# Attention values of two heads side by side in TensorE's column halves

## The reference

```
h  = rms_norm(x) * (1 + scale) + shift            # also for the context tokens
p  = h @ w_in                                     # 1024 x 2336, split among groups A, B, C, D
oA = softmax(qA kA^T / 8) vA                      # grouped keys: 4 query heads, 2 key/value heads
oB = softmax(qB kB^T / sqrt(96)) vB               # latent attention, 4 heads
oC = softmax over a window of +-128 tokens, the context keys and a sink logit, grouped keys
oD = softmax(qD kD^T / 8 + bias of a neighbourhood) vD
x  = x + gate * rms_norm(concat(oA, oB, oC, oD) @ w_out)
```

## Time and profile before

| | |
|---|---|
| median of 3 runs | 3002.4 us |
| profiled execution, its own time | 2995.0 us |
| its span | 2993.2 us |
| TensorE busy | 2667.0 us (89%), 13395 instructions |
| weight loads busy | 1353.2 us (45%) |
| VectorE busy | 1127.2 us (38%) |
| ScalarE busy | 576.0 us (19%) |
| GpSimd busy | 389.7 us (13%) |
| mean granted TensorE clock | 0.951 |
| from HBM and to it | 219 GB/s over the span |

### The profile page before, as it was taken

One profiled execution on the slowest core, in us unless ns is written; L12 is line 12 of the kernel. 1 busy time (PEld: TensorE's weight loads), 2 busy tenths in 40 slices (PEclk: granted clock), 3 DMA queues, 4 the chain that ended last, 5 costly groups with the idle time before them and its releaser, 6 DMA issues. The chain is left out here.

```text
span 2993.2 us, 44262 instructions
## 1 busy us (share of the span) xinstructions
PE 2667.0 (89%) x13395; PEld 1353.2 (45%) x13396; DVE 1127.2 (38%) x3287; ACT 576.0 (19%) x1309; POOL 389.7 (13%) x312
## 2 busy tenths in 40 slices
PE   7999989896899999999997598999978999899994
PEld 3576665653433333333332266666633333333331
DVE  3443361523433333333332653451524232333323
ACT  2222231311011111111111331331311111111111
POOL 1000001001012222222221200001010112122121
PEclk9999999997999999999998799999989999999997
DMA  7120203014577998999993502102137799998983
GB/s 273 43 88 29 100 28 127 13 43 162 217 242 254 357 332 287 325 321 333 328 362 88 194 1 88 70 30 111 36 137 282 293 395 393 384 402 288 384 329 105
DMA packets 104978, 619.26 MB, mean 207 GB/s; under 512 B 22832, under 2 KB 23088, under 8 KB 64688
## 3 DMA queue, kind: packets, MB, share of 16 engines
q1 hardware_dynamic: 71184, 530.30, 44.9%
q0 software_dynamic: 33696, 87.63, 12.0%
HBM read 578.84 MB, written 77.99 MB: 219 GB/s over the span
## 5 line engine op out<-in xcount | busy, mean ns | idle before, releaser
L1518 PE MATMUL ps<-wgu,xT 128*64 128x512 f32 x3584 | 810.9, 606 | 49.8 <-DMA wgu<-in_exp_gu 33.0
L1518 PEld LDWEIGHTS ps<-wgu,xT 128*64 128x64 f32 x3584 | 255.5, 139 | 510.1 <-issue 498.4
L1527 PE MATMUL ps<-wd,hiddenT 128*64 128x512 f32 x1824 | 418.3, 600 | 11.3 <-issue 10.3
L624 PE MATMUL ps<-w_in,hT 128*128 128x512 f32 (+5 forms) x1152 | 371.4, 482 | 14.8 <-PEq L381 4.0
L1447 POOL DMA_INDIRECT ffn_rows<-Y,six x114 | 182.5, 1601 | 1119.2 <-issue 649.7
L1700 DVE TENSOR_TENSOR hidden<-silu,ps 128x256 f32<-128x256 f32 x112 | 47.2, 421 | 713.3 <-ACT silu L1636 713.3
L624 PEld LDWEIGHTS ps<-w_in,hT 128*128 128x128 f32 x1152 | 218.2, 197 | 157.2 <-issue 137.8
L1527 PEld LDWEIGHTS ps<-wd,hiddenT 128*64 128x64 f32 x1824 | 123.8, 137 | 225.3 <-issue 224.3
L1636 ACT ACTIVATE silu<-ps 128x256 f32<-128x256 f32 x112 | 43.1, 384 | 807.1 <-PE ps L1518 807.1
L1694 DVE TENSOR_SCALAR Y<-ps,wc 128x512 f32<-128x512 f32 x114 | 85.6, 751 | 198.0 <-PE ps L1527 198.0
L1631 ACT ACTIVATE Y<-ps,wc 128x512 f32<-128x512 f32 x114 | 78.4, 688 | 415.7 <-PE ps L1527 415.7
(11 more groups left out here) (470 smaller groups left out, 2915.6 us busy)
## 6 DMA issues: line engine op xcount, KB each, us to landing
wgu<-in_exp_gu SPq DMA_DIRECT2D x128, 2048.0 KB, 13.5
wd<-in_exp_d SPq DMA_DIRECT2D x128, 1024.0 KB, 12.8
ada_start<-in_ada_w SPq DMA_DIRECT2D x8, 1024.0 KB, 7.9
w_in<-in_w_in SPq DMA_DIRECT2D x4, 2048.0 KB, 10.1
w_in<-in_w_out SPq DMA_DIRECT2D x4, 2048.0 KB, 12.6
aw_0A<-in_ada_w SPq DMA_DIRECT2D x6, 1024.0 KB, 5.4
aw_0B<-in_ada_w SPq DMA_DIRECT2D x6, 1024.0 KB, 4.8
aw_0C<-in_ada_w SPq DMA_DIRECT2D x6, 1024.0 KB, 4.9
```

The source lines that it names most:

```text
L624: last = pe.matmul(pp[i % 2][:, at:at + c1 - c0], hT[:, k, i * P:(i + 1) * P], wg[g % 2][:, k, c0:c1], start=(k == 0), stop=(k == KD - 1))
L1518: last = pe.matmul(ps[h * HB:(h + 1) * HB, 0, :], xT[:, k, h * HB:(h + 1) * HB], wgu[w[h]][:, k, :], start=(k == 0), stop=(k == KD - 1))
L1527: last = pe.matmul(ps[h * HB:(h + 1) * HB, 1 + c, :], G[:, f, h * HB:(h + 1) * HB], wd[w[h]][:, f, c * 512:(c + 1) * 512], start=(f == 0), ...
```

## The change

Units are reordered so that two heads of the same query tile follow each other, and each two make a pair `w`. `values(w)` treats both: V is stationary (64 columns), the turned probabilities move (128 columns), and the two heads go to the two column halves, that is to partitions 0 to 63 and 64 to 127 of one bank. The output so has head columns on partitions and query tokens along the row, which is the form that the output projection reads. The inverse sums lie one per partition (query token); they are spread by two more products (a broadcast column stationary, the identity moving), copied by ScalarE to RB, and VectorE multiplies and writes to `oT`, which is held for all tiles. PT has four buffers in place of two; PR takes the storage of R. In `project_out` the turns and their copies go. The host reorders rows of `w_out` to fit the order of heads in A and C.

```diff
+    units = [(2 * p + side, q) for p in range(2) for q in range(nt) for side in range(2)]
+    pairs = [(units[2 * w][0] // 2, units[2 * w][1]) for w in range(NU // 2)]
...
+        PR, PT = R, sb("PT", [P, 4, 768])
+        RB = sb("RB", [P, P])
...   in turn_probs(u):
-                    s_o.wait(pe, u - 1)
+                    if u % 2:
+                        s_o.wait(pe, u // 2)
...
-                def values(u):
-                    s_pa.wait(pe, local[u])
-                    s_pd.wait(pe, u + 1)
-                    c0 = kv_of(units[u][0]) * HD
-                    for c in range(lo(u) // P, 6):
-                        last = pe.matmul(ps[:, 5 + 2 * (u % 2), 256:256 + HD], PT[:, u % 2, c * P:(c + 1) * P],
-                                         V[:, key_tile(u, c), c0:c0 + HD], start=(c == lo(u) // P), stop=(c == 5))
+                def values(w):
+                    q = pairs[w][1]
+                    s_pa.wait(pe, local[2 * w + 1])
+                    s_pd.wait(pe, 2 * w + 2)
+                    for c in range(lo(2 * w) // P, 6):
+                        for side in range(2):
+                            c0 = kv_of(units[2 * w + side][0]) * HD
+                            pe.matmul(ps[side * HD:(side + 1) * HD, 7, 256:256 + P], V[:, key_tile(2 * w, c), c0:c0 + HD],
+                                      PT[:, (2 * w + side) % 4, c * P:(c + 1) * P], start=(c == lo(2 * w) // P), stop=(c == 5))
+                    s_inv.wait(pe, 2 * w + 2)
+                    for side in range(2):
+                        last = pe.matmul(ps[side * HD:(side + 1) * HD, 7, 384:512], st[:, 5, 2 * w + side:2 * w + side + 1].broadcast_to([P, HD]),
+                                         v.ident, start=True, stop=True)
                     last.then_inc(s_pv.sem, 1)
...   TensorE's loop, before turn_probs(u):
-                    if u:
-                        values(u - 1)
+                    if u and u % 2 == 0:
+                        values(u // 2 - 1)
...   ScalarE's loop:
+                for w in range(NU // 2):
+                    exps(2 * w + 1)
+                    if w:
+                        inverse_rows(w - 1)          # copy of ps[:, 7, 384:512] to RB
+                    probs(2 * w)                     # the copy to PT, as before
+                    probs(2 * w + 1)
+                    if 2 * w + 2 < NU:
+                        exps(2 * w + 2)
...   VectorE's loop, after maximum(u + 1):
-                    if u:
-                        divide(u - 1)
+                    inverse(u)                       # waits for exps(u): in C the sum with the sink; reciprocal
+                    if u and u % 2 == 0:
+                        out(u // 2 - 1)
+                def out(w):
+                    p, q = pairs[w]
+                    s_rb.wait(dve, w + 1)
+                    dve.tensor_tensor(oT[:, out0 // P + p, q * P:(q + 1) * P], RB[:, :], ps[:, 7, 256:384],
                                       ALU.mult).then_inc(s_o.sem, 1)
...   project_out, TensorE (turn(i) and, on ScalarE and VectorE, evac(i) are taken out):
-                turn(0)
...
-                    if i + 1 < nt:
-                        turn(i + 1)
-                            last = pe.matmul(ps[:, 2 * (i % 2) + n, :], oT[:, i % 2, k, :], w[n][:, k, 0:512],
+                            last = pe.matmul(ps[:, 2 * (i % 2) + n, :], oT[:, k, i * P:(i + 1) * P], w[n][:, k, 0:512],
```

More of the change, by code:

```diff
@@ L137, in build @@
                 for g in range(4):
-                    mixer(env, l, g, nt, hT, wg, o_tok)
-                project_out(env, l, nt, o_tok, wg)
+                    mixer(env, l, g, nt, hT, wg, oT)
+                project_out(env, l, nt, oT, wg)
             if stop == ("mix", l):
@@ L510, in mixer @@
     s_sc, s_max, s_exp, s_pt = S("scores"), S("negated_maximum"), S("exponentials"), S("probs_turned")
-    s_pa, s_pd, s_pv, s_o, s_sx = S("probs_by_act"), S("probs_by_dve"), S("weighted_values"), S("out_written"), S("sink_exp")
-    units = [(h, q) for h in range(4) for q in range(nt)]
+    s_pa, s_pd, s_pv, s_o, s_inv = S("probs_by_act"), S("probs_by_dve"), S("weighted_values"), S("out_written"), S("inverse_sums")
+    s_rb = S("inverse_rows")
+    units = [(2 * p + side, q) for p in range(2) for q in range(nt) for side in range(2)]
     NU = len(units)
+    pairs = [(units[2 * w][0] // 2, units[2 * w][1]) for w in range(NU // 2)]
     def lo(u):
@@ L721, in _ @@
                         scores(u + 1)
-                    if u:
-                        values(u - 1)
+                    if u and u % 2 == 0:
+                        values(u // 2 - 1)
                     turn_probs(u)
-                values(NU - 1)
+                values(NU // 2 - 1)
             @block.scalar
@@ L770, in exps, with probs, inverse_rows @@
                                    accum_out=st[:, 2, u:u + 1]).then_inc(s_exp.sem, 1)
[L772 to L775, removed]
+                def probs(u):
                     if lo(u) < 512:
                         s_pt.wait(act, u + 1)
-                        s_pv.wait(act, u - 1)
-                        act.copy(PT[:, u % 2, lo(u):512], ps[:, 4 + 2 * (u % 2), lo(u):512]).then_inc(s_pa.sem, 1)
+                        s_pv.wait(act, u // 2 - 1)
+                        act.copy(PT[:, u % 4, lo(u):512], ps[:, 4 + 2 * (u % 2), lo(u):512]).then_inc(s_pa.sem, 1)
+                def inverse_rows(w):
+                    s_pv.wait(act, w + 1)
+                    s_o.wait(act, w)
+                    act.copy(RB[:, :], ps[:, 7, 384:512]).then_inc(s_rb.sem, 1)
+                exps(0)
+                for w in range(NU // 2):
[6 more added lines that the diff above has]
+                        exps(2 * w + 2)
+                inverse_rows(NU // 2 - 1)
             @block.vector
@@ L892, in maximum, with inverse @@
                     ins.then_inc(s_max.sem, 1)
-                def divide(u):
-                    s, q = units[u]
-                    s_pv.wait(dve, u + 1)
+                def inverse(u):
+                    s_exp.wait(dve, u + 1)
                     den = st[:, 2, u:u + 1]
@@ L917, in _ @@
                         maximum(u + 1)
-                    if u:
-                        divide(u - 1)
+                    inverse(u)
+                    if u and u % 2 == 0:
+                        out(u // 2 - 1)
                     s_pt.wait(dve, u + 1)
-                    s_pv.wait(dve, u - 1)
-                    dve.tensor_copy(PT[:, u % 2, 512:768], ps[:, 5 + 2 * (u % 2), 0:256]).then_inc(s_pd.sem, 1)
-                divide(NU - 1)
+                    s_pv.wait(dve, u // 2 - 1)
+                    dve.tensor_copy(PT[:, u % 4, 512:768], ps[:, 5 + 2 * (u % 2), 0:256]).then_inc(s_pd.sem, 1)
+                out(NU // 2 - 1)
                 steps.append(n[0])
@@ L963, in project_out @@
     s_w = [S(f"w_out_loaded{n}") for n in range(2)]
-    s_row, s_t, s_ea, s_ed = S("gate_row_loaded"), S("turned"), S("turned_by_act"), S("turned_by_dve")
+    s_row = S("gate_row_loaded")
     s_mm, s_sq, s_ms, s_rstd, s_x, s_step = S("products"), S("squares"), S("mean_square"), S("rstd"), S("x_updated"), S("dve_step")
@@ L1013, in _ @@
             def _(act):
[L1014 to L1019, removed]
                 for i in range(nt):
-                    if i + 1 < nt:
-                        evac(i + 1)
                     s_mm.wait(act, i + 1)
@@ L1062, in _ @@
                     dve.tensor_tensor(v.xs[:, i, :], v.xs[:, i, :], add[:, :], ALU.add).then_inc(s_x.sem, 1)
-    for s, k in ((s_w[0], 16), (s_w[1], 16), (s_row, 16), (s_t, nt), (s_ea, nt), (s_ed, nt), (s_mm, nt), (s_sq, nt), (s_ms, nt), (s_rstd, nt),
+    for s, k in ((s_w[0], 16), (s_w[1], 16), (s_row, 16), (s_mm, nt), (s_sq, nt), (s_ms, nt), (s_rstd, nt),
                  (s_x, nt), (s_step, counts[0]), (s_mod, 1), (s_mt, 1), (s_mc, 1), (s_cs, 16)):
@@ L1891, in layout @@
     order[base:base + 544] = base + np.r_[0:192, 512:544, 192:384, 384:512]
+    rows = np.arange(D)
+    for base in (GROUPS[0][4], GROUPS[2][4]):
+        rows[base:base + 256] = base + np.array(perm)
     small = np.zeros((L, P, S_W), np.float32)
@@ L1916, in layout @@
         "x": f["x"][0], "ctx": f["ctx"][0], "cvec": cvec, "consts": consts, "consts16": consts16, "small": small,
-        "ada_w": ada, "w_in": f["w_in"][:, :, order], "w_up": f["b_w_kv_up"], "bias": bias, "w_out": f["w_out"],
+        "ada_w": ada, "w_in": f["w_in"][:, :, order], "w_up": f["b_w_kv_up"], "bias": bias, "w_out": f["w_out"][:, rows],
         "router_w": f["router_w"], "sh_gu": sh.reshape(L, P, KD * 2 * FD),
```

26 lines of the change are left out of this document (6 added, 20 removed).

## The result

The changed kernel takes 2921.2 us in the median of 4 runs (2917.0 to 2927.8); in the same comparison the kernel before takes 3002.4 (2998.0 to 3002.9). The ratio is 0.974, with a 95% interval of 0.9724 to 0.9755, which is 74 to 83 us off. The profiled execution took 2924.6, 70.4 less than the one before (2995.0), where the sum of terms had 64.3. That pair of traces is the fairer test of the sum, since all its terms were read from a trace.

The account below looks back on a forecast made before the run. TensorE was taken to bound the eight attention loops. Terms 32+12.2+5.2+8.5+6.4 = 64.3 us off the profiled 2995.0 give 2930.7; set against the median, 7.4 higher, 2938, with an 8-in-10 range of 2922 to 2967.

Parts of the forecast that it names:

- V block: Value products of a pair of units: 14 two-pass waves, 1.53 us, plus border, 1.79 us where it was 2x1.29.
- the border: Price per value block of entering and leaving the half-wide form: 0.26 to 0.28 us, bounds 0 and 0.4.
- A and B: Four attention-loop groups: 8 pairs each save 6.3 us plus 1.7 of waits, 8.0 a group, 32 in all.
- scattered waits: In A, 2.1 us, 0.13 a unit, of values for the copy of turned probabilities; 1.7 expected to go.
- the 0.25 of slack: In A, VectorE's chain to its copy takes 1.7 us against TensorE's cover of 1.95: no wait.
- rival 2: A wait of 0.5 us a pair replaces the saving in A and B too, context pairs win nothing: 2967; 17%.
- D: Two attention-loop groups with bias subtraction: VectorE's copy late by 0.51 us a pair; 6.1 saved a group, 12.2 for two.
- C: Two attention-loop groups with mask subtractions: waits for VectorE average 1.03 us a pair; 2.6 saved a group, 5.2 for two.
- The named chain: In C, VectorE's masks, reduction, minimum, sum, reciprocal and copy: 2.7 us middle tiles, 2.25 outer, against cover of 1.3 to 1.6.
- Context units of layer 0: Short latency-set units in the attention loops: one wait for the copy instead of two; 8.5 us saved, bounds 0 and 12.
- Projection: Output projection: turning of token rows goes, 5.2 us between products plus some 1.2 at layer 0's start; 6.4 us.
- rival 3: The border costs nothing and loads are hidden across it: 80 pairs win 0.26 us, 85 off, 2917; 8%.

Follow-up runs that it names:

- e1b: Changed kernel with all value products of the first head, then all of the second, instead of alternating per key tile: 2969.5 us, ratio 0.9903.
- e3b: Changed kernel with ScalarE copying all of every odd unit's turned probabilities and VectorE only those of even units: 2909.1 us, ratio 0.9708.
- e6: Changed kernel with ScalarE's RB copy moved ahead of the odd unit's exponentials, VectorE still copying for both units: 2918.5 us, ratio 0.9732.
- e2b: Kernel before with only the units in the new order; values, division and projection as before: 2999.1 us, ratio 0.9993.
- e0b: Changed kernel again, with a bit mask for a remainder in the experts' loop, as base of the experiments: 2919.7 us, ratio 0.973.

## Why the prediction was right

By its own steps:

- **V block, 1.79 us a pair.** Measured 1.68, and 0.09 before and 0.06 behind: 1.83. The halves do run at once: two passes 0.007 us apart, a wave every 0.109. e1b, with 2.60 us and the time of the kernel before in the loops of layer 1, shows what the block costs where they mostly do not. Waves are 0.109, as taken from the turns, and the border is 0.30 for 0.26 to 0.28, in the same three pieces that were read from L294: 0.09 ahead (0.09), 0.15 inside (0.14), 0.06 behind (0.05). The pair comes to 5.73 for 5.69. So 0.30 us is what going into the half-wide form and out of it costs here. Both halves use all 128 rows, and behind the first wave (0.16) no gap for a load shows between the passes of L690, which start 0.109 us apart, wave by wave. Where only one half is busy, e1b, a pass costs 0.109 as well, so the loads are hidden in either form.
- **A and B.** 8.0 us a group expected; 7.4 and 7.3 in layer 1. The steady part gives 8 x 0.75 = 6.0 of it (6.3 expected). The other term, 1.7 from 2.1 us of scattered waits, had its source wrong: in the trace before, the value blocks of A start 3.24 us apart in all the steady part, without any wait, and what waits there are stand at the end, 0.68 for each of the last two units. Start and tail together gave 1.4, so that this term was near its size by luck. No wait took the place of the saving: the 0.25 of slack before VectorE's copy held, and rival 2 with it fell.
- **D.** 6.1 a group expected, 6.5 measured. The wait for VectorE's copy is there, 0.38 a pair and not 0.51; the period is 6.11 for 6.20. e3b takes that wait away and D loses 2.
- **C.** 2.6 a group expected, 2.8 measured in layer 1; waits 5.9 us in all for 8.2. The named chain is the cause: e3b shortens it and C gains, e6 removes the only other candidate that VectorE's timeline shows and C gains 0.6 us in layer 1, no more than equal kernels differ.
- **Context units of layer 0.** This term was mis-sized: 8.5 expected, 15.2 measured (61.6 to 46.4), nearly all of the difference between 64.3 and 70.4. The text's own working had it: 3.0 to 3.5 us a pair for 3.5 to 4.4; it measures 2.6 to 3.2. I then took 1.5 off each of A, B and C, less than the working gave (16 pairs at a mean of 0.7 are 11), and gave no reason for it; and the pairs came out shorter than the working. e2b shows that the order of units gives 2 us of this gain at most, and the rows beside it show one wait for copies in place of two. That this is all of it, and what the side-by-side passes add, is argued and not shown: e1b leaves context pairs as they were.
- **Projection.** 6.4 expected, 6.7 measured. Layer 1 gave 2.5 for 1.7, layer 0 4.2 for 4.7. The turns between products were priced rightly: a token tile takes 13.73 us for 14.61. What was missed is the start: it gained 0.8 us in layer 1, where nothing was expected, and 0.7 in layer 0 for 1.2. The first tile is held by the second half of the output weights, in layer 0 too. In e6, where the clock stays at 1.00 at this place (below), TensorE waits for them:

```profile
586.13 6.28 PE L1020 MATMUL ps<-w_in,oT 128*128 128x512 f32 x14 [1.19 <-DMA w_in<-in_w_out]
```

  In the changed kernel a lower clock takes 1.7 us there and this wait is gone, and the block takes 88.78 us for e6's 88.55.
- **Sum.** Latent queries 24.0 a layer, 48.0 (49.4 expected), context 15.2, projection 6.7: 69.9 of the 70.4 between the two profiled executions.
- **The number.** Of the 17 us between the forecast of 2938 and the median, the terms explain 6. The median lies outside the 2925 to 2955 of the forecast itself, and nearer to rival 3's 2917, whose mechanism (a border that costs nothing) the trace refutes with 0.30 us. So the mechanism was right and the size on the low side; that 2922 as a lower end is missed by 0.8 us and not by more is partly chance.

The medians are further apart than the traces, 81 and 79 us in two comparisons. Some of it is scatter: the rest of the span spreads over 18 us among the seven executions with the change. One piece is regular. In both executions without the change the second expert's products in layer 1 begin after a wait of 9.3 us, for which the trace shows no releaser; in all seven with it the wait is 2.9 to 4.1. Before, and changed:

```profile
2324.59 9.02 PE L1518 MATMUL ps<-wgu,xT 128*64 128x512 f32 x32 [9.26 <-issue]
```
```profile
2251.33 8.57 PE L1513 MATMUL ps<-wgu,xT 128*64 128x512 f32 x32 [3.44 <-issue]
```

This stage is identical in both programs and lies some 110 us behind the projection. It is a gain of 5 to 6 us (already within the 70.4 of the traces, where other parts of the rest took it back) that no step of the prediction has and that no experiment here explains; e1b has it too, whose loops in layer 1 take as long as those before, so it does not come from faster loops there. It stays open, and so does what is left between 70 and 79.

## What to carry to other kernels

When a product has few output columns and many rows to move, let the narrow operand be stationary and put two such products in alternation into the column halves (here 1.83 us a pair where two units took 2.58): look for a pass form of the kernel that already does it, and read the distance between its starts. Write the products of the halves alternately in the program; with twelve passes a half, one half after the other gave it all back here (loops of layer 1: 219.8 us in e1b, 219.6 before; with four it changed nothing, 0.81 a block in both). Before that, add up the chain of each other engine against TensorE's new, shorter period: where the chain is longer (C), first take from the waited engine what another can do, then look at which instruction in whose queue is late next, and move only that; the same move tried earlier was worth nothing here (e6: loops of 437.9 for 437.4).

## What the hardware showed that I had not expected

- The clock. At the start of the projection in layer 0 the granted clock is 0.90 over 577.2 to 578.7, 0.50 over 578.8 to 581.7, and 1.00 from 582.0, after TensorE had been idle for 2.0 us, from 575.2 on, itself at 1.00:

```profile
577.20:578.70 1.50, 1.49 (x4) 0.71 (x5) 0.28 (x1) 0.00 (x0) 0.00 (x0) 0.90 0.69 213
578.80:581.70 2.90, 2.90 (x5) 1.30 (x4) 0.00 (x0) 0.00 (x0) 0.00 (x0) 0.50 1.06 408
582.00:588.00 6.00, 6.00 (x15) 2.66 (x14) 0.00 (x0) 0.00 (x0) 0.00 (x0) 1.00 0.48 161
```

  The passes from 578.20 to 582.05 take 3.85 us where five of them take 2.15 at 1.00 (0.43 each from 582.05 on), 1.7 lost, nearly all of it in time that TensorE would have spent waiting for weights (e6 above). It is not a result of the change: the kernel before also shows 0.50 at the same place, while TensorE turns rows:

```profile
616.00:618.40 2.40, 2.40 (x13) 2.36 (x12) 0.88 (x2) 0.59 (x1) 0.00 (x0) 0.50 0.92 290
```

  e0b has 0.50 too, over 575.1 to 578.4. But e6 and e1b, with the same 2.0 us of idle time ahead of L1012 (2.01 and 2.00), stay at 1.00 there, and so does layer 1 of the changed kernel (2.02). What decides is open.
- Order between halves. In e1b passes for one column half start ahead of passes for the other that stand before them in the program, by three passes and no more: in blocks of 24, 20 and 16 value passes alike, the first pass of the other half starts when three of the half before it are left, though its own half had been free for up to 0.93 us.
